# Two residual blocks on one core: evacuating earlier where stages meet, and local attention on three of four key blocks

## The chip, the cores and the metric

The kernel runs on one core of a Trainium2 chip. The metric is the device time of one execution in microseconds, lower is better. A core has TensorE (PE: matmuls; its weight loads are shown apart as PEld), VectorE (DVE), ScalarE (ACT), GpSimd (POOL) and SyncE (SP), each with its own queue of instructions, tied together by semaphores. Here SP issues every large DMA. All data is float32 or float32r.

## The reference

Two blocks for 256 tokens of width 2048. The first has two layers of gated convolution, differential attention with 6 heads and attention on 256 memory tokens with 4 heads. The second, cut to what the change touches:

```python
def second_block(x, c, ...):
    c_act = silu(c)
    mod = c_act @ w_mod + b_mod            # 2048 x 12288: shifts, scales and gates
    h = rms_norm(x, mix_norm_pre) * (1 + sc1) + sh1
    x = x + g1 * rms_norm(token_mixer(h), mix_norm_post)
    h = rms_norm(x, ffn_norm_pre) * (1 + sc2) + sh2
    x = x + g2 * rms_norm(conv_ffn(h), ffn_norm_post)

def token_mixer(h, ...):
    q_a, k_a, v_a, q_b, k_b, v_b, gk, og_b, g_a, g_b = split(h @ w_in)
    # 16 query heads on 4 key heads of width 64; a query sees the 128 keys up to its own position
    o_a = sliding_window_attention(rope(q_a), rope(k_a), v_a, sinks)
    o_b = rms_norm(gated_linear_attention(q_b, k_b, v_b, gk)) * silu(og_b)
    return (sigmoid(g_a) * (o_a @ w_br_a) + sigmoid(g_b) * (o_b @ w_br_b)) @ w_out
```

With 256 tokens the window makes four blocks of 128 queries by 128 keys. The block of the first queries with the last keys is masked out as a whole.

## The kernel before

Activations lie with features on partitions, 128 to a tile, and the 256 tokens along the free axis. The weights, with the modulation matrix most of the 557 MB moved, are read from HBM once and never kept, so the kernel is a stream of **units**: 512 KB of weight, as a rule 512 rows by 256 columns. Each float32 operand is split into a rounded high part and a remainder, and three of the four products are formed: a matmul of 512 columns takes the high weights against both parts of the input, one of 256 columns the low weights against its high part.

A unit passes through four queues. SP loads it into one of 5 buffers `RAW` (L358). ACT copies it, rounded, to `WH` (`act_split`, L540) once the unit four earlier is done. DVE subtracts for `WL` (`dve_split`, L549). PE runs 16 matmuls (L468 and L473; in stages with the tokens on PSUM's partitions 12 matmuls, L415 to L417). There are 4 buffers of `WH` and of `WL`. So when unit w ends, ACT and DVE prepare unit w+4.

Units make **pairs** of output tiles and pairs make **stages**, one for each group of weight columns, in the order mem0, mem1 (keys and values of the memory), then for each layer l qkv, heads_a, heads_b, heads_c, out, then q_a, gk, kv_a, q_b, k_b, v_b0, v_b1, og, g_a, g_b, branch_a, branch_b, mix_out, up0, down0, up1, down1. At a pair's end ACT copies the part made with the input's remainder out of PSUM (`HIGH`, L806) and DVE adds it (`evacuate`, L941 to L964). Both stand behind the split of unit w+4 on their queues.

A stage whose input is another stage's result needs it as `XH`, high part and remainder, in four **input chunks** of four tiles: a copy on ACT (`act_input_chunk`, L1125 or L1131) and a subtraction on DVE (`dve_input_chunk`, L1142 or L1150). There is one `XH`. A chunk is overwritten when the last unit that reads it is done, and `Stage.inside` says how many chunks are made between the last units of the stage before.

Smaller work rides beside the stream at fixed units: attention heads in heads_a to heads_c, 8 turns of local attention in q_b to v_b1 (two query heads a turn), linear attention in og and g_a. The modulation matrix is used up by 192 **modulation steps** on DVE (`dve_modulation`, L1948), each with a load of 512 KB through the same five buffers; `MOD_STEPS` lists the stages and how many steps each has, spread evenly over its units. The order of every queue is that of the Python program, written out by hand.

In a local turn, PE rotates the two query heads and the key head (`pe_rotate`, L1668 to L1671: products with signed permutations), computes the scores of 256 queries by 256 keys (L1239), transposes the probabilities (L1251) and the values (L1255), and multiplies them (L1272). DVE adds the mask (L1327).

## Time and profile before

| | |
|---|---|
| median of 3 runs | 2576.82 us (2576.81 to 2580.57) |
| the profiled execution | 2574.52 us, of which the span is 2572.8 us |
| PE busy, and with weight loads | 2532.5 us (98%), 2169.0 us (84%) |
| DVE, ACT, POOL busy | 1940.7 us (75%), 1297.0 us (50%), 10.8 us |
| DMA | 556.64 MB, mean 216 GB/s |
| granted TensorE clock, mean | 0.998 |

PE counts as busy from a matmul's start to its modelled end, so the few idle stretches are read off the order of time. A row of the timeline gives the start in microseconds from the span's start, a duration, and in brackets how long the engine was idle before it and what ended that.

### The profile page before, as it was taken

Reading aid. Unit: us, or ns where it says so; the run is one execution under the profiler, and the core shown is the slowest. Engines: PE = TensorE matmul, PEld = TensorE weight load, DVE = VectorE, ACT = ScalarE, POOL = GpSimd, SP = SyncE. Lnnn points to the kernel's source line nnn. Section 1 sums busy time; section 2 is a strip of 40 time slices with the busy share of each in tenths; the row PEclk is TensorE's granted clock in tenths of the full one; section 3 lists DMA queues with packets and bytes.
Section 4 is the critical chain, followed back from the end, with each engine's and each line's share of the span. In section 5 each row is a group of like instructions: output and inputs, shape, how many; then the busy total and the mean of one; then the engine's idle time right before and its main releaser. Section 6 shows DMA issues by size and latency. Waiting matters only on the chain.

```text
span 2572.8 us, 35319 instructions
## 1 busy us (share of the span) xinstructions
PE 2532.5 (98%) x13936; PEld 2169.0 (84%) x13936; DVE 1940.7 (75%) x2769; ACT 1297.0 (50%) x1758; POOL 10.8 (0%) x62
## 2 busy tenths in 40 slices
PE   7999999999999999999999999999999999999998
PEld 6888888888888878888788888888888888888886
DVE  6977776887777678676676877886888887788855
ACT  7544556554455555444445554544644443444443
POOL 0000000000000100000000000000000000000000
PEclk9999999999999999999999999999999999999999
DMA  8797454778755466755566888887466668967654
GB/s 277 223 300 246 150 168 152 244 262 282 236 154 166 153 234 221 232 158 152 161 200 209 254 282 275 271 280 266 139 195 191 190 216 301 287 193 204 201 191 140
DMA packets 526519, 556.64 MB, mean 216 GB/s; under 512 B 17409, under 2 KB 453762, under 8 KB 526226
## 3 DMA queue, kind: packets, MB, share of 16 engines
q1 hardware_dynamic: 526354, 554.38, 68.8%
q8 instruction: 110, 1.80, 0.3%
q14 instruction: 55, 0.45, 0.1%
HBM read 552.22 MB, written 2.10 MB: 215 GB/s over the span
## 4 chain that ended last, share of the span: by engine, by line
PE 92%; DVE 5%; ACT 1%; issue 1%; DMA 0%; DVEq 0%; SPq 0%; ACTq 0%
PE ACC L468 45%; PE ACC L473 22%; PE ACC L415 6%; PE ACC L416 6%; PE ACC L417 6%; DVE WL L549 2%; PE SC L1239 1%; PE OU L1272 1%; PE SC L1251 1%; PE SC L1280 1%; DVE XH L1150 1%; DVE XH L1142 0%; ACT WH L540 0%; DVE PR L1574 0%; DVE RAWMOD L1948 0%
## 5 line engine op out<-in xcount | busy, mean ns | idle before, releaser
L468 PE MATMUL ACC<-XH,WH 128*128 128x512 f32 x5296 | 1688.8, 400 | 21.0 <-DVE XH L1150 15.2
L540 ACT ACTIVATE WH<-RAW 128x1024 fp32r<-128x1024 f32 (+1 forms) x852 | 896.9, 1057 | 1089.0 <-PE ACC L473 757.5
L549 DVE TENSOR_TENSOR WL<-RAW,WH 128x1024 fp32r<-128x1024 f32 (+1 forms) x852 | 1032.2, 1220 | 511.9 <-ACT WH L540 510.8
L473 PEld LDWEIGHTS ACC<-XH,WL 128*128 128x128 f32 x5296 | 996.6, 188 | 235.3
L473 PE MATMUL ACC<-XH,WL 128*128 128x256 f32 x5296 | 1043.3, 278 | 0.0
L468 PEld LDWEIGHTS ACC<-XH,WH 128*128 128x128 f32 x5296 | 812.7, 189 | 41.0 <-issue 18.5
L1948 DVE SCALAR_TENSOR_TENSOR RAWMOD<-RAWMOD,CSILU 128x1024 f32<-128x1024 f32 x192 | 234.1, 1219 | 1.5 <-DMA RAWMOD<-in_w_mod_t 1.5
L415 PE MATMUL ACC<-WH,XH 128*128 128x512 f32 x384 | 151.9, 396 | 3.6 <-DVE WL L549 3.6
L416 PE MATMUL ACC<-WL,XH 128*128 128x512 f32 x384 | 149.7, 390 | 0.0
L417 PE MATMUL ACC<-WH,XH 128*128 128x512 f32 x384 | 149.6, 390 | 0.0
L415 PE MATMUL ACC<-WH,AH 128*128 128x512 f32 x352 | 137.4, 390 | 0.0
L417 PE MATMUL ACC<-WH,AH 128*128 128x512 f32 x352 | 137.1, 389 | 0.0
L416 PE MATMUL ACC<-WL,AH 128*128 128x512 f32 x352 | 137.0, 389 | 0.0
L415 PEld LDWEIGHTS ACC<-WH,XH 128*128 128x128 f32 x384 | 72.1, 188 | 22.0 <-issue 7.6
L806 ACT ACTIVATE HIGH<-ACC 128x512 f32<-128x512 f32 (+1 forms) x171 | 89.6, 524 | 0.0
L417 PEld LDWEIGHTS ACC<-WH,XH 128*128 128x128 f32 x384 | 72.1, 188 | 15.3
L416 PEld LDWEIGHTS ACC<-WL,XH 128*128 128x128 f32 x384 | 72.1, 188 | 14.4
L417 PEld LDWEIGHTS ACC<-WH,AH 128*128 128x128 f32 x352 | 66.1, 188 | 13.8
L415 PEld LDWEIGHTS ACC<-WH,AH 128*128 128x128 f32 x352 | 66.1, 188 | 13.5
L416 PEld LDWEIGHTS ACC<-WL,AH 128*128 128x128 f32 x352 | 66.1, 188 | 13.5
L1297 ACT ACTIVATE PROB<-PROB,NM 128x256 f32<-128x256 f32 x80 | 39.7, 498 | 61.3 <-DVE NM L1336 61.3
L941 DVE TENSOR_TENSOR PR<-ACC,HIGH 128x512 f32<-128x512 f32 x64 | 43.8, 685 | 2.1 <-ACT HIGH L806 2.1
(287 smaller groups left out, 1436.3 us busy)
## 6 DMA issues: line engine op xcount, KB each, us to landing
RAW<-in_w_in SPq DMA_DIRECT2D x408, 512.0 KB, 4.5
RAWMOD<-in_w_mod_t SPq DMA_DIRECT2D x192, 512.0 KB, 4.8
RAW<-in_w_up SPq DMA_DIRECT2D x176, 512.0 KB, 4.7
RAW<-in_w_out SPq DMA_DIRECT2D x96, 512.0 KB, 5.5
RAW<-in_w_down SPq DMA_DIRECT2D x88, 512.0 KB, 4.9
RAW<-in_w_mem_kv SPq DMA_DIRECT2D x32, 512.0 KB, 5.9
RAW<-in_w_branch_gla SPq DMA_DIRECT2D x32, 512.0 KB, 5.0
RAW<-in_w_branch_attn SPq DMA_DIRECT2D x16, 512.0 KB, 4.9
```

What stands on the lines that cost most here:

```text
L415: pe.matmul(bank, x, high[:, kc], start=tile == 0, stop=False)
L416: pe.matmul(bank, x, low[:, kc], start=False, stop=False)
L417: mm = pe.matmul(bank, operand[:, tile, T + b * P:T + b * P + P], high[:, kc], start=False, stop=tile == WK * stage.per_pair - 1)
L468: return pe.matmul(bank, k.WH[:, w % RING, kc, cols], x, start=tile == 0, stop=False)
L473: return pe.matmul(bank[:, 0:T], k.WL[:, w % RING, kc, cols], x[:, 0:T], start=False, stop=tile == tiles - 1)
L540: act.activation(k.WH[:, slot, :, 0:width], k.RAW[:, r % RAWS, :, 0:width], ACT.Copy).then_inc(k.hi_ready, 1)
L549: dve.tensor_tensor(k.WL[:, slot, :, 0:width], k.RAW[:, k.plan.unit_load[unit] % RAWS, :, 0:width], k.WH[:, slot, :, 0:width].bitcast(F32) ...
L806: act.activation(k.HIGH[:, first:stage.tiles], k.ACC[:, bank + first:bank + stage.tiles, T:2 * T], ACT.Copy).then_inc(k.high_ready, 1)
L941: chain.link(dve.tensor_tensor(dst, low, high, ALU.add))
L1150: last = dve.scalar_tensor_tensor(out=k.XH[:, f, T:2 * T], in0=prep.source(k)[:, f, :], scalar=prep.gain(k)[:, f:f + 1], in1=hi, op0=ALU.m ...
L1297: last = act.activation(k.PROB[:, g, :], source, ACT.Exp, bias=k.NM[:, g:g + 1], scale=scale, accum_out=k.SM[:, g:g + 1])
L1948: dve.scalar_tensor_tensor(out=raw, in0=raw, scalar=1.0, in1=k.CSILU[:, half * MOD_COLS:(half + 1) * MOD_COLS], op0=ALU.mult, op1=ALU.mult ...
```

## The change

1. **Early evacuation.** `evacuated_early` picks pairs whose `HIGH` and `evacuate` now come ahead of the split of unit w+4: the last pair of mem0, mem1, out0, g_b, branch_a, branch_b and kv_a, and both pairs of the last turn of heads_c. In that turn one DVE split (`held_split`) moves behind the last gate product, and a convolution product (L1580) moves one unit later.
2. **Moved work.** ACT's squares of `x` and DVE's sums of them come three units earlier in mem0. The activation of `c` with its two table loads (`act_small`) goes from mem0 to mem1, and `dve_small` from behind mem0 to behind mem1. Modulation steps keep clear of the first or last units of ten stages.
3. **Input order.** branch_b and mix_out take their input rows in the order 2, 3, 0, 1. branch_a reads only half of `XH`, so the chunks for rows 2 and 3 are made within branch_a at its units 8 and 10.
4. **Local attention.** Scores, mask, exponentials, transposes and values leave out the empty block. Keys are rotated every second turn, values transposed every fourth, from where they lie, without the copy `VS` (dropped in differential attention too).

```diff
 MOD_STEPS = [
-    ("mem1", 6), ("qkv0", 22), ("out0", 16), ("qkv1", 22), ("out1", 12), ("q_a", 8),
+    ("mem1", 3, 8, 12), ("qkv0", 25, 6, 40), ("out0", 16, 4, 27), ("qkv1", 22, 5, 40),
 ...
+LATE_FIRST = (2, 3, 0, 1)
+    by_name["branch_a"].then_first = 2
+    by_name["branch_b"].spots = by_name["mix_out"].spots = LATE_FIRST
 ...
+def held_split(stage, i, w):
+    return stage.beside == "mem" and i == MEM_T // 2 and w == 7
 ...
+def evacuated_early(stage, i, b, q):
+    if q < stage.per_pair - 1:
+        return False
+    final = i == stage.turns - 1 and b == stage.body - 1
+    mixing = stage.beside == "mem" and i == MEM_T // 2
+    return mixing or final and (stage.then is not None or stage.name == "kv_a")
 ...
                 dve_softmax(dve, k, stage, i, w, chain)
-                split_ahead(dve, k, stage, i, w, last, dve_split)
+                early = evacuated_early(stage, i, b, q)
+                if early:
+                    evacuate(i, b)
+                if not held_split(stage, i, w):
+                    split_ahead(dve, k, stage, i, w, last, dve_split)
 ...
-                if stage.name == "mem0" and (i, w) == (1, 2):
+                if stage.name == "mem1" and (i, w) == (0, 6):
                     act_small(act, k)
-                if stage.name == "mem0" and i == 1 and w in (3, 4):
+                if stage.name == "mem0" and i == 1 and w in (0, 1):
                     act.wait_ge(k.x_landed, 64)
-                    for c in (2 * w - 6, 2 * w - 5):
+                    for c in (2 * w, 2 * w + 1):
                         act_squares(act, k, 1, c)
 ...
+                if stage.name == "branch_a" and i == 2 and w in (0, 2):
+                    dve_input_chunk(dve, k, k.preps["ob"], w // 2)
 ...
 def pe_scores(pe, k, kind, u, m=None):
     pe.wait_ge(k.qk_ready, u + 1)
+    if kind == "win":
+        for c in range(2):
+            rows = slice(64 * c, 64 * c + 64)
+            for b in range(2):
+                mm = pe.matmul(k.SC[:, c, window_block(b)], k.QN[rows, 0, P * b:P * b + P],
+                               k.KN[rows, 0, 0:P * (b + 1)], start=True, stop=True)
+        mm.then_inc(k.scores_ready, 1)
+        return
 ...
+def turned_blocks(kind):
+    if kind == "win":
+        return [(c, first, first) for c in range(2) for first in (0, P, 2 * P)]
 ...
+    if kind == "win":
+        for c in range(2):
+            out = k.OU[64 * c:64 * c + 64, 0, 0:T]
+            for kc in range(2):
+                v = k.VT[:, kc * P + 64 * m.parity:kc * P + 64 * m.parity + 64]
+                mm = pe.matmul(out[:, kc * P:], v, k.TURNED[:, c, kc * T:3 * P if kc else T],
+                               start=kc == 0, stop=kc == 1)
 ...
+def values_turned(kind, n):
+    if kind == "diff":
+        return D_V + n
+    return V_A + n // 4 if kind == "win" and n % 4 == 0 else None
 ...
-    pe.matmul(k.SC[:, 0, 0:T], k.ROT[:, :], k.PR[:, O_A + j, :], start=True, stop=True)
-    keys = k.PR[:, K_A + j // 4, :]
-    pe.matmul(k.SC[:, 0, T:2 * T], k.DUP[:, parity, :], keys, start=True, stop=True)
-    pe.matmul(k.SC[:, 1, 0:T], k.DUPROT[:, parity, :], keys, start=True,
-              stop=True).then_inc(k.rotated, 1)
+    mm = pe.matmul(k.SC[:, 0, 0:T], k.ROT[:, :], k.PR[:, O_A + j, :], start=True, stop=True)
+    if j % 2 == 0:
+        keys = k.PR[:, K_A + j // 4, :]
+        pe.matmul(k.SC[:, 0, T:2 * T], k.DUP[:, parity, :], keys, start=True, stop=True)
+        mm = pe.matmul(k.SC[:, 1, 0:T], k.DUPROT[:, parity, :], keys, start=True, stop=True)
+    mm.then_inc(k.rotated, 1)
```

On PE, the second turn of local attention stands thus before; `ROT`, `DUP` and `DUPROT` are the permutations, and the dots are the stream's own matmuls:

```order
L1668 MATMUL SC<-PR,ROT 128x256
L1670 MATMUL SC<-PR,DUP 128x256
L1671 MATMUL SC<-PR,DUPROT 128x256
...
L1239 MATMUL SC<-KN,QN 128x256 x4
...
L1251 MATMUL SC<-IDENT,PROB 128x128 x8
L1255 MATMUL OU<-IDENT,VS 128x128 x2
...
L1272 MATMUL OU<-TURNED,VT 64x256 x4
```

and thus now:

```order
L1769 MATMUL SC<-PR,ROT 128x256
...
L1301 MATMUL SC<-KN,QN 128x128
L1301 MATMUL SC<-KN,QN 128x256
L1301 MATMUL SC<-KN,QN 128x128
L1301 MATMUL SC<-KN,QN 128x256
...
L1328 MATMUL SC<-IDENT,PROB 128x128 x6
...
L1350 MATMUL OU<-TURNED,VT 64x256
L1350 MATMUL OU<-TURNED,VT 64x128
L1350 MATMUL OU<-TURNED,VT 64x256
L1350 MATMUL OU<-TURNED,VT 64x128
```

Both key rotations and both value transposes are gone from this turn, two of the eight transposes of probabilities as well, and two of the four score and value matmuls are half as wide.

On DVE, the last units of heads_c and the first of out stand thus before (`PR<-ACC,HIGH` and `PR<-PR,RSTD` evacuate a pair, `WL<-RAW,WH` is a split, `XH<-PR,XH` an input chunk, `PR<-PR` the gate products L1584 and L1593):

```order
L1142 TENSOR_TENSOR XH<-PR,XH 128x4x256
L549 TENSOR_TENSOR WL<-RAW,WH 128x1024
L1584 TENSOR_TENSOR PR<-PR 128x1024
L1142 TENSOR_TENSOR XH<-PR,XH 128x4x256
L549 TENSOR_TENSOR WL<-RAW,WH 128x1024
L1142 TENSOR_TENSOR XH<-PR,XH 128x4x256
L549 TENSOR_TENSOR WL<-RAW,WH 128x1024
L941 TENSOR_TENSOR PR<-ACC,HIGH 128x512
L943 TENSOR_TENSOR PR<-PR,RSTD 128x512
L1593 TENSOR_TENSOR PR<-PR 128x512
L1142 TENSOR_TENSOR XH<-PR,XH 128x2x256 x2
L549 TENSOR_TENSOR WL<-RAW,WH 128x1024 x2
```

and thus now:

```order
L1189 TENSOR_TENSOR XH<-PR,XH 128x4x256
L564 TENSOR_TENSOR WL<-RAW,WH 128x1024
L1684 TENSOR_TENSOR PR<-PR 128x1024
L1189 TENSOR_TENSOR XH<-PR,XH 128x4x256
L564 TENSOR_TENSOR WL<-RAW,WH 128x1024
L1189 TENSOR_TENSOR XH<-PR,XH 128x4x256
L979 TENSOR_TENSOR PR<-ACC,HIGH 128x512
L981 TENSOR_TENSOR PR<-PR,RSTD 128x512
L1693 TENSOR_TENSOR PR<-PR 128x512
L564 TENSOR_TENSOR WL<-RAW,WH 128x1024
L1189 TENSOR_TENSOR XH<-PR,XH 128x2x256 x2
L564 TENSOR_TENSOR WL<-RAW,WH 128x1024 x4
```

One split, that of the next stage's fourth unit, has moved behind the evacuation and the gate product, so that both come one split earlier.

On DVE at the border of out0 and qkv1, before (`X<-X,SUM` ends the evacuation, `RAWMOD` is a modulation step):

```order
L549 TENSOR_TENSOR WL<-RAW,WH 128x1024
L1948 SCALAR_TENSOR_TENSOR RAWMOD,DERIVED<-RAWMOD,CSILU 128x1024
L1150 SCALAR_TENSOR_TENSOR XH<-X,PARAM,XH 128x256 x4
L549 TENSOR_TENSOR WL<-RAW,WH 128x1024
L1150 SCALAR_TENSOR_TENSOR XH<-X,PARAM,XH 128x256 x4
L549 TENSOR_TENSOR WL<-RAW,WH 128x1024
L1948 SCALAR_TENSOR_TENSOR RAWMOD,DERIVED<-RAWMOD,CSILU 128x1024
L953 TENSOR_TENSOR SUM<-ACC,HIGH 128x512
L964 TENSOR_TENSOR X<-X,SUM 128x512
L1150 SCALAR_TENSOR_TENSOR XH<-X,PARAM,XH 128x256 x4
```

and now:

```order
L564 TENSOR_TENSOR WL<-RAW,WH 128x1024
L1197 SCALAR_TENSOR_TENSOR XH<-X,PARAM,XH 128x256 x4
L564 TENSOR_TENSOR WL<-RAW,WH 128x1024
L1197 SCALAR_TENSOR_TENSOR XH<-X,PARAM,XH 128x256 x4
L991 TENSOR_TENSOR SUM<-ACC,HIGH 128x512
L1002 TENSOR_TENSOR X<-X,SUM 128x512
L564 TENSOR_TENSOR WL<-RAW,WH 128x1024
L1197 SCALAR_TENSOR_TENSOR XH<-X,PARAM,XH 128x256 x4
```

The modulation steps have left the border, and the evacuation stands ahead of the last split.

## Rows read from the trace of the kernel before

**Rows 1.** The page: busy time, chain by engine, groups of splits and modulation.

```profile
PE 2532.5 (98%) x13936; PEld 2169.0 (84%) x13936; DVE 1940.7 (75%) x2769; ACT 1297.0 (50%) x1758; POOL 10.8 (0%) x62
PE 92%; DVE 5%; ACT 1%; issue 1%; DMA 0%; DVEq 0%; SPq 0%; ACTq 0%
L1948 DVE SCALAR_TENSOR_TENSOR RAWMOD<-RAWMOD,CSILU 128x1024 f32<-128x1024 f32 x192 | 234.1, 1219 | 1.5 <-DMA RAWMOD<-in_w_mod_t 1.5
```

**Rows 2.** Timeline, PE: first matmul after each idle stretch between stages.

```profile
60.56 0.70 PE L468 MATMUL ACC<-XH,WH 128*128 128x512 f32 x2 [1.64 <-issue]
65.36 0.73 PE L468 MATMUL ACC<-XH,WH 128*128 128x512 f32 x2 [1.77 <-DVE XH L1150]
472.07 0.73 PE L468 MATMUL ACC<-XH,WH 128*128 128x512 f32 x2 [1.81 <-DVE XH L1142]
565.25 0.73 PE L468 MATMUL ACC<-XH,WH 128*128 128x512 f32 x2 [2.43 <-DVE XH L1150]
923.34 0.47 PE L415 MATMUL ACC<-WH,XH 128*128 128x512 f32 x1 [2.79 <-DVE WL L549]
1090.30 0.70 PE L1668 MATMUL SC<-PR,ROT 128*128 128x256 f32 x2 [0.38 <-DVE PR L946]
1638.80 0.70 PE L468 MATMUL ACC<-XH,WH 128*128 128x512 f32 x2 [1.69 <-issue]
1642.17 0.73 PE L468 MATMUL ACC<-XH,WH 128*128 128x512 f32 x2 [0.35 <-DVE XH L1142]
1740.54 0.47 PE L415 MATMUL ACC<-WH,XH 128*128 128x512 f32 x1 [0.82 <-DVE WL L549]
```

**Rows 3.** Timeline, PE: the pieces of one local turn, and what follows.

```profile
1117.60 0.60 PE L1668 MATMUL SC<-PR,ROT 128*128 128x256 f32 x2
1118.04 0.59 PE L1670 MATMUL SC<-PR,DUP 128*128 128x256 f32 x2
1127.35 1.14 PE L1239 MATMUL SC<-KN,QN 64*128 64x256 f32 x8
1128.42 0.50 PE L468 MATMUL ACC<-XH,WH 128*128 128x512 f32 x1
1136.88 1.04 PE L1251 MATMUL SC<-IDENT,PROB 128*128 128x128 f32 x8
1137.76 0.38 PE L1255 MATMUL OU<-IDENT,VS 128*128 128x128 f32 x2
1140.87 1.09 PE L1272 MATMUL OU<-TURNED,VT 128*64 128x256 f32 x8
```

**Rows 4.** Timeline, weight loads of the same score matmuls.

```profile
1127.34 0.74 PEld L1239 LDWEIGHTS SC<-KN,QN 64*128 64x128 f32 x8
```

**Rows 5.** Timeline, DVE and ACT at the borders.

```profile
63.64 1.66 DVE L1150 SCALAR_TENSOR_TENSOR XH<-Y,PARAM,XH 128x256 fp32r<-128x256 f32 x4
466.70 0.69 DVE L941 TENSOR_TENSOR PR<-ACC,HIGH 128x512 f32<-128x512 f32 x1
470.72 1.29 DVE L1142 TENSOR_TENSOR XH<-PR,XH 128x512 fp32r<-128x512 f32 x2 [1.22 <-ACT XH L1125]
560.34 0.69 DVE L953 TENSOR_TENSOR SUM<-ACC,HIGH 128x512 f32<-128x512 f32 x1
914.45 1.22 DVE L549 TENSOR_TENSOR WL<-RAW,WH 128x1024 fp32r<-128x1024 f32 x1
920.88 3.90 ACT L540 ACTIVATE WH<-RAW 128x1024 fp32r<-128x1024 f32 x4
```

**Rows 6.** Stretches: length, busy PE, PEld, DVE, ACT, POOL (count), clock, DMA share, GB/s.

```profile
10.00:20.00 10.00, 8.95 (x44) 7.77 (x44) 9.21 (x18) 9.29 (x17) 0.00 (x0) 1.00 1.10 353
111.92:225.97 114.05, 114.05 (x654) 98.84 (x653) 93.28 (x121) 51.79 (x58) 0.00 (x0) 1.00 0.87 284
152.00:172.00 20.00, 20.00 (x117) 17.47 (x116) 14.99 (x20) 9.30 (x10) 0.00 (x0) 1.00 0.94 310
1086.98:1303.49 216.51, 216.13 (x1155) 177.24 (x1153) 148.99 (x247) 104.35 (x174) 0.00 (x0) 1.00 0.53 160
```

More of the change, by code:

```diff
@@ L258, in place_modulation @@
     units = []
-    for name, steps in MOD_STEPS:
+    for name, steps, *stretch in MOD_STEPS:
         stage = by_name[name]
-        if isinstance(steps, tuple):
+        if not stretch:
             units += [stage.unit0 + i * stage.units + w for i in range(stage.turns) for w in steps]
             continue
-        length = stage.pairs * stage.per_pair // (2 if name == "mix_out" else 1)
-        units += [stage.unit0 + (2 * j + 1) * length // (2 * steps) for j in range(steps)]
+        first, length = stretch[0], stretch[1] - stretch[0]
+        units += [stage.unit0 + first + (2 * j + 1) * length // (2 * steps) for j in range(steps)]
     assert len(units) == MOD_BLOCKS * KT
@@ L459, in operands @@
             s, tile, tiles = q // 2, 2 * UK * (q % 2) + 2 * kc + h, 4 * UK
+            x = operand[:, tile]
         else:
             s, tile, tiles = h, UK * q + kc, UK * stage.per_pair
-        return (k.ACC[:, bank0 + s], operand[:, tile], s, tile, tiles, kc,
-                slice(h * P, h * P + P))
+            x = operand[:, UK * (stage.spots[q] if stage.inputs is not None else q) + kc]
+        return (k.ACC[:, bank0 + s], x, s, tile, tiles, kc, slice(h * P, h * P + P))
     def high(place, w):
@@ L792, in turn @@
                     act_decays(act, k, w)
-                if stage.name == "branch_a" and w == 2:
-                    act_gate_chunk(act, k, "g_b", G_B, ACT.Sigmoid, k.gb_ready, i)
+                if stage.name == "branch_a" and i < 2 and w in (1, 3):
+                    act_gate_chunk(act, k, "g_b", G_B, ACT.Sigmoid, k.gb_ready, 2 * i + w // 2)
                 if stage.name == "qkv1" and i > 0 and w == 2:
@@ L1033, in turn @@
                     dve_modulation(dve, k, n)
+                if stage.name == "branch_a" and i == 2 and w in (0, 2):
+                    dve_input_chunk(dve, k, k.preps["ob"], w // 2)
                 if last and b == stage.body - 1 and q < stage.inside and stage.then:
-                    dve_input_chunk(dve, k, k.preps[stage.then], q)
-            evacuate(i, b)
+                    dve_input_chunk(dve, k, k.preps[stage.then], stage.then_first + q)
+            if not early:
+                evacuate(i, b)
     stage_turns(stage, turn)
     if stage.then is not None:
-        for c in range(stage.inside, k.preps[stage.then].chunks):
+        for c in range(stage.then_first + stage.inside, k.preps[stage.then].chunks):
             dve_input_chunk(dve, k, k.preps[stage.then], c)
@@ L1166, with __init__ @@
 class Prep:
-    def __init__(self, first, free, chunks, norm, scaled, source, gain, shift, chunk, ready):
+    def __init__(self, first, free, chunks, norm, scaled, source, gain, shift, chunk, ready, free_at,
+                 order):
         self.first, self.free, self.chunks = first, free, chunks
+        self.free_at, self.order = free_at, order
         self.norm, self.scaled, self.source = norm, scaled, source
@@ L1310, in act_copy_turned @@
     else:
-        last = act.activation(k.TURNED[:, :, :], k.SC[:, :, :], ACT.Copy)
-    if kind != "mem":
+        width = 3 * P if kind == "win" else 2 * T
+        last = act.activation(k.TURNED[:, :, 0:width], k.SC[:, :, 0:width], ACT.Copy)
+    if values is not None:
         last = act.activation(k.VT[:, :], k.OU[:, 1, 0:T], ACT.Copy)
```

165 lines of the change are left out of this document (101 added, 64 removed).

## The prediction, made before the changed kernel ran

> **What bounds the kernel.** I read the page's busy shares and its chain first [rows 1]: PE is busy for 98% of the span, and 92% of the chain that ended last runs over PE. A cut elsewhere is worth nothing unless PE waits for it. Two things can pay: instructions taken off PE, and the stretches in which PE stands still. For the second I read PE's timeline for rows with a bracket. Between the first matmul and the last there are few, all where one stage's result is the next one's input. Those that the change touches are in [rows 2], and their brackets sum to 1.64 + 1.77 + 1.81 + 2.43 + 2.79 + 0.38 + 1.69 + 0.35 + 0.82 = 13.68 us. The idle time at the start, at the end, before q_a and before up0 is not touched, and I leave it.
>
> **Local attention on PE.** Over the local turns PE is busy 216.13 of 216.51 us [rows 6], so what goes from PE there goes from the time. In [rows 3]:
> - Key rotations: one product of 256 columns takes 1118.04 - 1117.60 = 0.44 us. Two go in each of four turns: 8 x 0.44 = 3.5 us.
> - Transposes: eight take 1137.76 - 1136.88 = 0.88, so 0.11 each. Two of probabilities go in each of 8 turns, two of values in each of 6, 28 in all: 3.1 us.
> - Scores: four matmuls take 1128.42 - 1127.35 = 1.07 us, or 0.27 each with the start of the group in it. The rows on one half of the partitions run beside those on the other, which without that start would be half of 0.44, 0.22. Two of the four become half as wide: one matmul's worth, 0.22 a turn, 1.8 us in all.
> - Values: the group of the same size (1.09 against 1.14), by the same count 1.8 us.
>
> Sum 10.2 us. The narrow matmuls are the uncertain part. If a matmul of 128 columns costs as much as one of 256, scores and values give nothing and 6.6 us are left; at 0.27 for each they give 4.3 and the sum is 11.0. I take 10.2, since [rows 4] shows the eight weight loads of the scores inside 0.74 us, less than the 1.07 of their matmuls, so that a load doesn't set the pace.
>
> The Trainium skill speaks against this ("TensorE: Matmul & The Clock Gate", section "LDWEIGHTS (loading the stationary operand)"): a load's time goes with its columns and not its rows, about 107 ns for 128. Eight in a row would take 0.86 us however narrow the moving side is, and scores and values would gain nothing. The 0.74 us in [rows 4], with the last load's own duration in it, disagree with that here. It is a rival below.
>
> On DVE a local turn loses the copy of the values, and mask, maximum and scaling become smaller, while one reduction becomes two. DVE is busy for 149 of 216.5 us there [rows 6], so either sign costs nothing. PE's waits in a turn need the scores' inputs three units after the turn begins and the probabilities three units later. With less in front on DVE and ACT both come earlier. In differential attention nothing changes on PE.
>
> **The borders.** qkv0 has 40 units and takes 114.05 us [rows 6], of which the keys and values of the memory are some 2.6, so a unit takes PE 2.79 us. A split takes 1.0 on ACT and 1.22 on DVE, an input chunk of four tiles 1.7 on DVE and as much on ACT, a modulation step 1.22 on DVE [rows 1, 5]. Where PE would have come is the start in [rows 2] less its bracket.
> - mem0 to mem1 (1.64 + 1.77): the first input chunk waited for ACT, which had the table loads, the activation of c and the squares in the last five units, and the second for DVE, which did the sums in front of it and ended it at 63.64 + 1.66 = 65.30 [rows 5]. Now ACT has in each of the last units only a split and a chunk, 1.0 + 1.7 = 2.7 of 2.79 us, and DVE, with a backlog of some 3 us from the sums and an evacuation, ends chunks 0 to 3 about 0.5, 0.5, 2.4 and 1.0 us ahead of PE. All 3.4 go. ACT now waits for x three units earlier, but the loads of x stand in front of that of unit 10, and ACT has split unit 11 by then. Two table loads and three activations move to mem1's unit 6. The four buffers of splits hide them: a split begins three units, 8.4 us, before PE wants it and takes 2.2 on both engines, so some 6 us may come in between.
> - heads_0c to out0 (1.81): the evacuation at 466.70 releases silu, gate product and the last chunk, which ends at 472.01 [rows 5]. One split less in front of it is 1.14, the pair before gives another 0.8 by its own early evacuation, and the chunk then stands behind the held split, whose 1.14 lie beside ACT's two copies. It ends near 470.1, PE comes at 470.3. I count 1.6.
> - out0 to qkv1 (2.43): three modulation steps (3.7 us) and a split leave the front of the evacuation at 560.34 [rows 5]. The last chunk, which ended at 565.2, ends near 560.9, and PE comes at 562.8. All of it goes.
> - heads_1c to out1 (2.79): here the split for out1's fifth unit was late. ACT had waited for silu, table and chunk and began four splits only at 920.88 [rows 5]. With the evacuation some 2 us earlier that split ends near 921.0, PE comes at 920.55. The held split, in [rows 5] done at 915.7, ends near 917.4, PE comes a unit before, at 917.8. 2.3 of 2.79 go; this is the tightest place.
> - kv_a to q_b (0.38): the evacuation is one split earlier. All goes.
> - branch_a to branch_b (1.69 + 0.35): the first two chunks are made eight and six units ahead, the other two have two more units each. All goes.
> - branch_b to mix_out (0.82): a modulation step and a split leave the front of the last evacuation, 2.4 us; the last chunk and ACT's splits behind it come as much earlier. All goes.
>
> Sum 3.4 + 1.6 + 2.4 + 2.3 + 0.4 + 2.0 + 0.8 = 12.9 us. Bounds: 13.7, all the brackets, and, if in each of the seven places 1 us stays, 6.
>
> **What is added.** The modulation steps stay 192, only their places change. The densest is qkv0: 25 steps in 34 units, 59 loads of 524 KB in 94.9 us, 326 GB/s. In [rows 6] the trace has 310 GB/s with a DMA share of 0.94 in that stage, and 353 at the start, where loads queue. At 310 the loads fall 4.9 us behind over the stretch, inside the 6 us that the buffers hold; so nothing, with a bound of 2 us. DVE has there 1.22 + 1.22 x 25/34 + 0.35 (evacuation) = 2.47 of 2.79 us. An early evacuation delays the split behind it by 1.4 us, with those same 6 us above it.
>
> **Sum.** 10.2 + 12.9 = 23.1 us off the profiled execution's 2574.52: 2551.4. The median of the runs stood 2.3 us above that execution, so the median after is near 2554.
>
> **Rivals.**
> - *The stalls move.* At mem0's end DVE has a split and a chunk in each unit, 1.22 + 1.66 = 2.88 us against PE's 2.79, and the held split has 0.3 us to spare. For it speaks that I walk queues with margins of 0.2 to 1 us, in seven places. Against it: the large terms (out0, branch_a, mem0) have over 0.5 us. With about 1 us left in each place the borders give 6, so 16 in all: 2561. With nothing gained at borders: 2566.5.
> - *Narrow matmuls save nothing.* A weight load sets the pace of scores and values: 3.6 us less, 2557.5. This is the skill's rule above; [rows 4] speaks against it.
> - *Slower: DMA can't feed the denser stretches.* In qkv0, out0, qkv1 and branch_b, 198 loads (104 MB) now fall in 119 units, 332 us, 313 GB/s on the mean. Each stretch may fall 6 us behind before PE waits. The gain of 23 is gone when the rate is below 104 / (332 + 4 x 6 + 23) = 274 GB/s, and at 265 the time is 2590. [rows 6] shows 310 in a stretch with loads no sooner wanted, so this is unlikely.
> - *The change doesn't do what it says.* The order of instructions shows the products gone and the evacuations moved; this could only be a hidden wait for a buffer, and is in the first rival.
>
> **Chances.** The forecast, 2551 to 2557: 0.76. Stalls move, 2557 to 2567: 0.15. Narrow matmuls: 0.06. Slower: 0.03. The range 2550.5 to 2563 reaches into the first rival; its low end is the upper bound of the gain (11.0 + 13.7: 2552.1) and 1.6 more, since the 2.3 us between a profiled execution and a median need not be the same (the runs before lie 3.8 apart). About 0.2%, 5 us, is what can be told from no change: faster by more 0.95, within 0.02, slower 0.03.
>
> **What would show it.** The stretch from q_b to v_b1 near 206 us instead of 216.5 with PE busy throughout, of which four turns lose 1.8 us each, two 0.9 and two 0.7; out of the nine brackets at most one or two left, under 1 us each, the likeliest at out1's fourth or fifth unit; qkv0 as long as before, at 2.79 us a unit, though ACT waits more for DMA in it. I am wrong if a new bracket over 1 us stands before a first unit of a stage, if the local stretch is above 209 us, or if qkv0 is over 2 us longer.

## The result, and the profile after

The changed kernel takes 2549.76 us (median of 4 runs, 2549.31 to 2551.72), before 2577.9 in the same comparison: ratio 0.9891, 95% interval 0.9874 to 0.9908, so 1.1% faster. The forecast was 2554.0 with a range from 2550.5; the time lies 0.74 us below that end. The sign was right, the gain was larger than forecast: 23.1 us forecast, 25.1 between the two profiled executions (2574.52 and 2549.41), 28.1 between the medians. Both gaps need a reason.

The page after, busy time, chain and modulation group, the lines that answer to [rows 1]:

```profile
PE 2521.2 (99%) x13892; PEld 2162.1 (85%) x13892; DVE 1927.7 (76%) x2745; ACT 1291.4 (51%) x1752; POOL 10.4 (0%) x63
PE 98%; DVE 1%; DMA 0%; ACT 0%; issue 0%; DVEq 0%; SPq 0%
L2053 DVE SCALAR_TENSOR_TENSOR RAWMOD<-RAWMOD,CSILU 128x1024 f32<-128x1024 f32 x192 | 233.9, 1218 | 0.5 <-DMA RAWMOD<-in_w_mod_t 0.4
```

The chain runs over PE for 98% where it was 92%. In place of the nine brackets of [rows 2] the list of all of PE's waits has only those at the start, before q_a and before up0. Columns: who waited for whom, us in total, times, longest.

```profile
PE ACC L483 <- DVE XH L1197: 11.1, 1, 11.1
PE SC L747 <- DVE PR L952: 4.2, 2, 2.9
PE SC L747 <- DVE WL L564: 0.7, 1, 0.7
PE ACC L456 <- DVE XH L963: 0.2, 1, 0.2
```

The stretches that answer to [rows 6] (same columns): local attention, 10.6 us shorter and PE busy throughout, and qkv0, as long as it was though DMA moves 290 GB/s in it for 284.

```profile
1076.00:1281.90 205.90, 205.90 (x1111) 169.66 (x1109) 139.42 (x235) 98.39 (x168) 0.00 (x0) 1.00 0.56 169
108.69:222.75 114.06, 114.06 (x654) 98.85 (x653) 95.58 (x130) 52.34 (x60) 0.00 (x0) 1.00 0.87 290
```

Measured from the first weight matmul of a stage to that of the next, the stages differ by (us, after less before; those left out by 0.02 or less):

```
mem0 -0.85   mem1 -2.45   out0 -1.82   qkv1 -2.71   out1 -2.84
q_a  +1.18   kv_a -1.57
q_b  -3.02   k_b  -2.64   v_b0 -2.37   v_b1 -2.59
branch_a -1.58   branch_b -0.70   mix_out -1.05   up0 -0.26
```

Borders and local attention account for nearly all. Three of these hold something else, the granted clock. In the kernel before, PE is at half clock (0.50 in the column PEclk, 1.2 GHz for 2.4) for 3.41 us around q_a's beginning and for 3.41 in kv_a; after, for 6.82 us around q_a's beginning and not in kv_a:

```profile
985.00:990.00 5.00, 5.00 (x23) 3.84 (x21) 3.59 (x6) 2.38 (x4) 0.00 (x0) 1.00 0.98 314
992.26:999.08 6.82, 6.10 (x23) 5.31 (x24) 6.51 (x16) 4.90 (x8) 0.00 (x0) 0.50 0.47 156
```

And at the start the first matmuls run at half pace: a pair of 512 columns takes 0.86 us start to start, later 0.46. Before, the pace doubles behind 13.77, after, behind 15.99. That is 0.94 us in mem0's first unit (4.19 and 5.13). The column PEclk reads 1.00 there in both profiles; the half pace is read from the matmuls' starts. PE's timeline, before, then after:

```profile
12.49 1.05 PE L468 MATMUL ACC<-XH,WH 128*128 128x512 f32 x2
13.77 0.69 PE L468 MATMUL ACC<-XH,WH 128*128 128x512 f32 x2
```

```profile
15.13 1.05 PE L483 MATMUL ACC<-XH,WH 128*128 128x512 f32 x2
16.26 0.63 PE L483 MATMUL ACC<-XH,WH 128*128 128x512 f32 x2
```

So the borders gave 0.85 + 0.94 + 2.45 (mem) + 1.82 + 2.71 + 2.84 + 0.38 (in front of q_b) + 1.58 + 0.70 + 1.05 = 15.3 us, for brackets of 13.68, and local attention 10.62 - 0.38 = 10.2.

### The profile page after: what moved, and what is told of

The parts are those of the page before. It is cut to its first block, busy times and chain, and to the rows that moved or that the text cites. A ratio compares the mean times of both kernels' runs of the same rounds, so it can differ in the third digit from the quotient of the medians.

```text
span 2547.6 us, 35203 instructions
## 1 busy us (share of the span) xinstructions
PE 2521.2 (99%) x13892; PEld 2162.1 (85%) x13892; DVE 1927.7 (76%) x2745; ACT 1291.4 (51%) x1752; POOL 10.4 (0%) x63
## 4 chain that ended last, share of the span: by engine, by line
PE 98%; DVE 1%; DMA 0%; ACT 0%; issue 0%; DVEq 0%; SPq 0%
PE ACC L483 49%; PE ACC L488 24%; PE ACC L429 7%; PE ACC L431 7%; PE ACC L430 7%; PE SC L1310 1%; PE OU L1361 1%; PE SC L1328 1%; PE SC L1369 1%; PE ACC L456 0%; PE OU L1833 0%; PE SC L1301 0%; PE OU L1350 0%; PE OU L1498 0%; DVE X L931 0%; DMA RAW<-in_w_mem_kv 0%
## 5 line engine op out<-in xcount | busy, mean ns | idle before, releaser
L483 PE MATMUL ACC<-XH,WH 128*128 128x512 f32 x5296 | 1688.8, 400 | 11.2 <-DVE XH L1197 11.1
L1388 ACT ACTIVATE PROB<-PROB,NM 128x256 f32<-128x256 f32 (+1 forms) x80 | 38.0, 477 | 55.9 <-DVE NM L1435 55.9
```

The costliest lines, as they stand in the source:

```text
L483: return pe.matmul(bank, k.WH[:, w % RING, kc, cols], x, start=tile == 0, stop=False)
L1388: last = act.activation(probs, source, ACT.Exp, bias=k.NM[:, g:g + 1], scale=scale, accum_out=k.SM[:, g:g + 1])
```

## The experiments

All were timed in five rounds beside the kernel before. Each execution lists its mean granted clock, and times go with it: 10 of 59 executions of before show 0.998 and take 2574.5 to 2575.2 us, 13 show 0.997 and take 2576.6 to 2578.1, 34 show 0.996 and take 2577.9 to 2580.7, and 2 show 0.994 and take 2582.8 and 2583.2. Where a few us matter I compare executions of one clock.

### The two halves alone

Local attention of the changed kernel in the kernel before; the changed kernel with the local attention of before; both kernels again. The edits are parts of the diff above, or none.

> The kernel before with the local attention of the changed kernel and none of the moves at stage borders. Mine: the stretch from q_b to v_b1 falls from 216.51 to about 206.3 us (the 0.38 us stop in front of q_b stays), all other stages and all eight other stops stay; 10.2 us less than before. Rival A (the parts help each other, for example a shorter local turn only pays because the borders are free): less than 8 us. Rival B (the 2 us by which the change gave more than forecast lie in local attention, outside the profiled PE rows): more than 12 us between the medians.

> The changed kernel with the local attention of before: only the moves at borders and the modulation steps. Mine: the nine stops go, whose brackets are 13.68 us; each stop also costs some 0.2 us beside its bracket (the profile draws a matmul 0.39 us long though the next one starts 0.23 us after it, and the first matmul after a stop takes 0.31 for 0.23), so 15.5 us less at equal clock. Rival A (forecast as made: brackets alone, and 0.7 of them stay): 12.9 us. Rival B (gains are those of the stage table without any clock correction): 14.5 us. Local attention stays at 216.1 us.

Local attention alone: 2568.62 us, ratio 0.9968 (0.9956 to 0.9981). Borders alone: 2563.61, ratio 0.9948 (0.9935 to 0.9962). The stretches from q_b to v_b1, local part alone, then borders alone:

```profile
1092.84:1299.37 206.53, 206.17 (x1110) 169.68 (x1109) 139.44 (x235) 98.37 (x168) 0.00 (x0) 1.00 0.56 168
```

```profile
1078.36:1294.23 215.87, 215.87 (x1155) 177.09 (x1153) 148.94 (x247) 104.34 (x174) 0.00 (x0) 1.00 0.53 161
```

216.51 - 206.53 = 10.0 us, and the 0.36 of PE's idle time in front of q_b is left. With borders alone, out0, qkv1, branch_a, branch_b and mix_out are as long as in the changed kernel within 0.01 us. They lost 7.86 us for brackets of 1.81 + 2.43 + 1.69 + 0.35 + 0.82 = 7.10.

out1 is the exception, and there both expectations missed. With borders alone one of the nine stops is left, in out1's fifth unit, and the stage is 0.85 us longer than in the changed kernel. With local attention alone the stop there is 2.13 us, not 2.79.

```profile
913.61 0.47 PE L429 MATMUL ACC<-WH,XH 128*128 128x512 f32 x1 [0.60 <-DVE WL L564]
```

So the local half gives some 0.65 us at this border. The way leads over GpSimd and DVE. At the end of heads1c GpSimd builds the window mask, which the change makes smaller (384 columns for 512), and DVE does six convolution steps beside it. They take 3.55 us in before and with borders alone, 2.9 with local attention alone and in the changed kernel. DVE's timeline, before, then after:

```profile
892.81 3.55 DVE L1574 SCALAR_TENSOR_TENSOR PR<-CU,PARAM,PR 128x256 f32<-128x256 f32 x6
885.05 2.89 DVE L1674 SCALAR_TENSOR_TENSOR PR<-CU,PARAM,PR 128x256 f32<-128x256 f32 x6
```

In the first layer, where GpSimd does nothing at that time, six such steps take 2.46 us in before. That GpSimd's work is what slows them fits all of this; no run changes the mask alone.

By stages (mem0 corrected for its start, as above) borders alone give 14.7 us and local attention alone 10.0 + 0.7 = 10.7, together 25.4 for the 15.3 + 10.2 of the changed kernel. So the halves add up, and neither needs the other but for this 0.65 us. The medians give 14.3 and 9.3 us. That they are 0.4 and 1.4 us short is within what half-clock stretches do: the profile of local attention alone has 20 us of them, that of borders alone 10, the two of before 7 and 17.

> The kernel before, unchanged, for a second profile. It differs from its first profile only in where TensorE is granted half its clock. Mine: stage lengths are the same within 0.1 us wherever the granted clock is 1.0, and the stretches at 0.5 have moved, come or gone; they explain the distance between the profiled execution (2574.52 us) and the median of the runs (2577.9): about 3 us, two half-clock stretches of 3.4 us more than the first profile had. Rival: the distance lies in the frame around the span (before the first and after the last instruction), with the clock's stretches the same.

> The changed kernel, unchanged, for a second profile. Mine: all nine stops are gone again; q_a's extra 1.2 us and kv_a's missing 1.6 us, which follow the stretches at half clock, come out another way; everything else stays within 0.1 us. Rival: q_a is longer and kv_a shorter by the change itself, and the same numbers return.

Before, again: 2579.18 us, ratio 1.0006 (0.9997 to 1.0015), profiled execution 2579.31 with a span of 2577.6. After, again: 2551.99 (4 runs, 2549.34 to 2555.23), ratio 0.9901 (0.9887 to 0.9914), span 2547.7. The second profile of after repeats the first, q_a's half-clock stretch and all: my theory that it would come out another way fell, and the rival's numbers returned. What speaks against the rival are other profiles: borders alone and `dense` (below) have the same edits around q_a and kv_a, and there q_a takes 48.66 and 48.64 us for 48.91 and kv_a 27.69 for 26.14, with 3.41 us at half clock in each. Two of after's four runs are 5 us longer, at clock 0.996. The second profile of before has five half-clock stretches where the first has two, and differs in nothing else but the start (mem0 0.69 us longer): mem1, qkv1 and out1 are longer by 1.25, 1.56 and 1.53 us. One begins 1.2 us behind the end of the stop of 2.42 us in qkv1:

```profile
565.40:568.10 2.70, 1.10 (x6) 0.97 (x7) 2.48 (x5) 2.70 (x4) 0.00 (x0) 1.00 0.21 79
568.16:571.57 3.41, 3.41 (x13) 2.92 (x12) 3.41 (x5) 0.87 (x1) 0.00 (x0) 0.50 0.55 163
571.58:575.00 3.42, 3.42 (x18) 2.99 (x18) 2.76 (x5) 2.44 (x4) 0.00 (x0) 1.00 0.98 318
```

One begins at the end of out1's stop (926.56; PE goes on at 926.65), and one in mem1 0.6 us behind the end of its second stop (65.84):

```profile
66.40:69.81 3.41, 3.41 (x12) 2.93 (x11) 3.34 (x8) 1.90 (x4) 0.00 (x0) 0.50 0.50 153
```

The profile of local attention alone has one there too, 1.5 us behind that stop. None of the 12 profiles of kernels with the changed borders, other than those with the early evacuation or the squares undone (below), has a half-clock stretch at mem1, out0, qkv1 or out1's fifth unit. The frame around the span is 1.7 to 1.8 us in all profiles. So the 2.3 us that I had put between profile and median are half-clock stretches, and the stops that the change removes had been bringing some of them.

### Parts undone

> The changed kernel, but in local attention all scores and value products are 256 columns wide again (the values of the second key block are read from the wrong place, so the output is not the reference's; the number and size of the instructions is what counts). Key rotations, transposes, mask and borders stay as changed. Mine: 0.22 us for scores and 0.22 for values in each of eight turns, the stretch from q_b to v_b1 goes from 205.89 to 209.4, 3.5 us more. Rival (a weight load sets the pace, so narrow products save nothing): the stretch stays at 205.9.

```diff
-                mm = pe.matmul(k.SC[:, c, window_block(b)], k.QN[rows, 0, P * b:P * b + P],
-                               k.KN[rows, 0, 0:P * (b + 1)], start=True, stop=True)
+                mm = pe.matmul(k.SC[:, c, P * b:P * b + T], k.QN[rows, 0, P * b:P * b + P],
+                               k.KN[rows, 0, 0:T], start=True, stop=True)
 ...
-                mm = pe.matmul(out[:, kc * P:], v, k.TURNED[:, c, kc * T:3 * P if kc else T],
+                mm = pe.matmul(out, v, k.TURNED[:, c, kc * P:kc * P + T],
```

2557.49 us, ratio 0.9919 (0.9905 to 0.9932). The stretch of local attention:

```profile
1079.18:1288.46 209.28, 209.28 (x1111) 171.00 (x1109) 139.37 (x235) 98.60 (x168) 0.00 (x0) 1.00 0.55 166
```

3.38 us more than 205.90 in eight turns, 0.42 each; I had forecast 0.44. The rest of the difference of the medians is half-clock stretches. A narrow product is worth what its columns say. In the changed kernel the eight weight loads of a turn's scores stand inside 0.53 us (those of [rows 4] took 0.74), so they got faster with the products. Timeline, PE and PEld, the row that answers to L1239 of [rows 3], and its loads:

```profile
1114.22 0.93 PE L1301 MATMUL SC<-KN,QN 64*128 64x128 f32 x8
1114.22 0.53 PEld L1301 LDWEIGHTS SC<-KN,QN 64*128 64x128 f32 x8
```

The Trainium skill ("TensorE: Matmul & The Clock Gate", section "LDWEIGHTS (loading the stationary operand)") has a load's time go with its 128 columns whatever its rows. The loads of this group begin in pairs, one for each half of the partitions, 0.01 us apart, and the four pairs follow each other by 0.11 us: 0.53 less the last load's own 0.19 is 0.34, three such steps. So here that time holds for a pair of loads and not for each, and a pair of products of 128 columns, 0.11 us too, just keeps its pace. My rival had counted eight loads one behind the other.

> The changed kernel with every evacuation back behind the split of the unit, and no held split. Mine: stops come back where the prediction gave the early evacuation as the cause: out0 1.6 to 1.8 us, out1 2.0 to 2.8, q_b 0.38, together 4.5 to 5.5 with 0.2 for each; at qkv1 and mix_out, where modulation steps were taken away too, 0 to 1 each; mem0 and branch_a none. Sum about 6 us at equal clock. Rival (modulation steps and chunk order did the work, the early evacuation hides in slack): under 2 us.

```diff
 def evacuated_early(stage, i, b, q):
-    ...
+    return False
 def held_split(stage, i, w):
-    return stage.beside == "mem" and i == MEM_T // 2 and w == 7
+    return False
```

2559.13 us, ratio 0.9929 (0.9916 to 0.9941). The stops that came back, all of them:

```profile
468.66 0.50 PE L483 MATMUL ACC<-XH,WH 128*128 128x512 f32 x1 [1.80 <-DVE XH L1187]
918.13 0.47 PE L429 MATMUL ACC<-WH,XH 128*128 128x512 f32 x1 [2.13 <-DVE WL L564]
1088.44 0.70 PE L1765 MATMUL SC<-PR,ROT 128*128 128x256 f32 x2 [0.38 <-DVE PR L982]
```

out0, out1 and q_b, as expected, 4.3 us of brackets. out0 became 3.38 us longer for its 1.80, since a half-clock stretch began at 469.87. At mem0, qkv1, branch_a and mix_out nothing came back: there the other edits are enough by themselves.

> The changed kernel with the squares of x, their sums and the activation of c back where they were, in the last units of mem0 and in front of mem1. Mine: the two stops at mem0/mem1 come back, shorter than the 1.64 and 1.77 us of before by the evacuation that is still early: 2 to 3.4 us of brackets and 0.25 for each stop; nothing else moves but the stretches at half clock. Rival (the early evacuation alone had removed them): no stop over 0.3 us there and the same time.

```diff
-                if stage.name == "mem1" and (i, w) == (0, 6):
+                if stage.name == "mem0" and (i, w) == (1, 2):
                     act_small(act, k)
-                if stage.name == "mem0" and i == 1 and w in (0, 1):
+                if stage.name == "mem0" and i == 1 and w in (3, 4):
 ...
```

2553.97 us, ratio 0.991 (0.9896 to 0.9923). The stops of before return at full length although the evacuation is early, with a third behind them:

```profile
60.40 0.47 PE L483 MATMUL ACC<-XH,WH 128*128 128x512 f32 x1 [1.63 <-issue]
65.19 0.50 PE L483 MATMUL ACC<-XH,WH 128*128 128x512 f32 x1 [1.76 <-DVE XH L1197]
74.08 0.50 PE L483 MATMUL ACC<-XH,WH 128*128 128x512 f32 x1 [0.98 <-DVE XH L1197]
```

At clock 0.998 that is 2553.9 against 2549.4, 4.5 us. The squares, sums and activation of c, which this run moves back together, did all of this border.

> The changed kernel with the modulation steps of qkv0 to out1 and of g_b to mix_out spread evenly over their stages again, in the same numbers (the last units and those behind a border are no longer free of them). Mine: a step of 1.22 us stands again in front of the last evacuation; stops of 0.3 to 2.4 us come back at qkv1 and 0.3 to 0.8 at mix_out, 1 to 3 us together; out0 and out1 stay as changed, since their borders have no step in front. Rival (the steps' places don't matter once the evacuation is early): no stop, same time.

```diff
-    ("mem1", 3, 8, 12), ("qkv0", 25, 6, 40), ("out0", 16, 4, 27), ("qkv1", 22, 5, 40),
+    ("mem1", 3, 8, 12), ("qkv0", 25, 0, 40), ("out0", 16, 0, 32), ("qkv1", 22, 0, 40),
 ...
```

2553.66 us, ratio 0.9905 (0.9892 to 0.9919); the one run at 0.998 takes 2550.33, 0.9 more than the changed kernel. A stop of 0.55 us came back at qkv1 and none at mix_out: that stage is 0.30 us longer without idle time of PE at its border, and branch_a 0.27 shorter; what moved there is not known. At qkv1 PE comes at 556.9 and the last chunk ends at 555.76 + 1.67 = 557.4 (DVE's timeline), because one modulation step stands between split and chunk:

```profile
553.48 1.22 DVE L564 TENSOR_TENSOR WL<-RAW,WH 128x1024 fp32r<-128x1024 f32 x1
554.61 1.22 DVE L2053 SCALAR_TENSOR_TENSOR RAWMOD<-RAWMOD,CSILU 128x1024 f32<-128x1024 f32 x1
555.76 1.67 DVE L1197 SCALAR_TENSOR_TENSOR XH<-X,PARAM,XH 128x256 fp32r<-128x256 f32 x4
557.35 1.22 DVE L564 TENSOR_TENSOR WL<-RAW,WH 128x1024 fp32r<-128x1024 f32 x1
```

### More load, and stops by themselves

> The changed kernel with 30 instead of 25 modulation steps in qkv0's 34 units, and 17 instead of 22 in qkv1: 64 loads (33.5 MB) in 94.9 us, 353 GB/s wanted. Mine: the queue gives up to 350 GB/s when it is behind, as in the first 10 us of the kernel, so qkv0 stays at 114.06 us or grows by at most 1 us. Rival (the 310 GB/s seen in that stage before is its limit): the loads fall 13 us behind, less 6 to 8 us that the buffers hold, and qkv0 is 5 to 7 us longer. DVE has 2.65 of 2.79 us per unit and is not the limit.

```diff
-    ... ("qkv0", 25, 6, 40), ... ("qkv1", 22, 5, 40),
+    ... ("qkv0", 30, 6, 40), ... ("qkv1", 17, 5, 40),
```

2552.98 us, ratio 0.99 (0.9886 to 0.9913). Neither theory: qkv0 stays at 114.06, but heads0a behind it grows by 2.99, with two stops. The loads came at 316 GB/s for the 353 wanted (first row, over the 34 units), ACT waited 55.3 us for DMA in them (38.4 in the changed kernel), and the stops came just behind the stage's end:

```profile
124.60:219.00 94.40, 94.40 (x541) 81.67 (x540) 79.04 (x105) 40.59 (x43) 0.00 (x0) 1.00 0.93 316
...
227.11 0.70 PE L1369 MATMUL SC<-SQ,HALVES 128*128 128x512 f32 x1 [2.24 <-DVE SQ L1718]
234.24 0.49 PE L1310 MATMUL SC<-KN,QN 64*128 64x256 f32 x2 [0.41 <-DVE KN L1732]
```

By my estimate 3.6 of the 33.5 MB wanted in 94.9 us were late, 11 us at 316 GB/s, and the buffers hid all but 3. DVE was busy for only 79.04 of 94.40 us in the first row, so over the stage its own work was not the limit. But at the first stop PE waits for DVE, which had worked since 216.85 with hardly a break, and late loads and DVE's own work are not separated there. So denser steps do cost, and the change stops at most five steps short of it. The forecast's DMA rival needed under 274 GB/s; the rate here was above that.

> The changed kernel with nine stops added where it has none: in front of heads0a, b, c, heads1a, b, c, og, g_a and g_b, PE waits until GpSimd has done five small chained memsets, which begin when PE ends the stage before. Mine: each stage with a stop becomes longer by the stop's bracket and 0.2 to 0.3 us, and behind some of the nine stops a stretch at half the granted clock begins within 4 us, which costs 1.5 to 1.7 us more; about a third of them, so 3 such stretches, other ones in each execution. With brackets b the time grows by 9 x (b + 0.25) + 3 x 1.6. Rival A: a stop costs its bracket alone, 9 x b. Rival B: half-clock stretches come at fixed places (before q_a, in kv_a, up0) and not at added stops: 9 x (b + 0.25).

```diff
+def pe_stop(pe, k, name):
+    if name in STOPS:
+        pe.wait_ge(k.held, STOPS.index(name) + 1)
+def pool_stops(pool, k, names, chain):
+    for name in names:
+        pool.wait_ge(k.unit_done, k.plan.s[name].unit0)
+        for n in range(5):
+            chain.link(pool.memset(k.HOLD[:, :], 1.0))
+        pool.sem_inc(k.held, 1)
```

> The kernel with nine added stops, each made longer: 14 chained memsets on GpSimd instead of 5, so brackets of about 2.4 us (two of the nine 2.0 and 1.7) instead of 0.2 to 1.0. Mine now: it is the length of a stop that decides. Behind two to five of the nine a stretch at half clock begins within 4 us, each 1.5 us more, so the time is that of the changed kernel plus the brackets, nine times 0.17, and 3 to 7 us. Rival (the place decides: only stops that fall together with an input change or low-row work bring one): no half-clock stretch near the nine, as with the short stops, and the time is brackets plus 1.5 us.

```diff
-        for n in range(5):
+        for n in range(14):
```

Short stops: 2558.95 us, ratio 0.9926 (0.9914 to 0.9939). Long: 2580.14, ratio 1.0011 (1.0002 to 1.002). PE's waits in the one, then in the other:

```profile
PE ACC L483 <- POOLq L2221: 6.3, 9, 1.0
```

```profile
PE ACC L483 <- POOLq L2221: 20.5, 9, 2.6
```

The stages around the short stops grew by 7.75 us for brackets of 6.33: 0.16 us a stop beside its bracket. None of the nine is followed by a half-clock stretch; the three in that profile are at q_a, in kv_a and at up0, as in most. Of the nine long stops, two are. They begin 0.19 us behind the stop of 1.76 us in front of og, and within that of 2.56 in front of g_a:

```profile
1404.00:1405.30 1.30, 0.00 (x0) 0.00 (x0) 1.24 (x3) 1.28 (x3) 0.88 (x8) 1.00 0.77 201
1405.31:1408.72 3.41, 2.90 (x9) 2.52 (x10) 1.03 (x2) 3.23 (x4) 0.29 (x3) 0.50 0.66 222
1408.73:1412.00 3.27, 3.27 (x20) 2.83 (x19) 0.62 (x1) 3.23 (x4) 0.00 (x0) 1.00 0.01 4
```

Stages grew by 24.88 us for 20.5 of brackets, so 4.4 beside them: 9 x 0.16 and 2.9 for the two stretches. So added stops do bring such stretches, against the rival. Length seems to matter: stops up to 1.0 us brought none of nine, those of 1.76 to 2.56 two of nine. One profile of each is thin for a rate, but the other executions point the same way: all eleven with long stops show a mean clock of 0.994 or less, all five with short ones 0.996 or 0.997. The stop of 1.76 brought one while the six of 2.13 and 2.56 ahead of it did not, so length is not all that decides.

The Trainium skill (same page, section "HAM oscillation — how this bites in real kernels") describes a matmul stream that loses its full clock because PE waits for loads between its pieces. These rows agree in kind, for a stream that is over 98% busy.

### Filling the idle time

> The changed kernel with matmuls of constants that nobody reads while PE would stand still: 44 (128 columns each) before mem0 and 24 behind out1, in front of q_a. Mine: the granted clock follows what PE does, so mem0 starts at full clock (1.4 to 2.5 us less) and the stretch at half clock at q_a goes (3.1 us less); 4.5 to 5.5 us less than the changed kernel, and the runs lie closer together. Rival (the half-clock stretches come at fixed times, or from the wait and not from idleness): mem0 no shorter, q_a's stretch stays; 0.

```diff
+    pe_keep_warm(pe, k, s["mem0"], 44)
     pe_stage(pe, k, s["mem0"])
 ...
+    pe_keep_warm(pe, k, s["q_a"], 24)
     for f in range(4):
         pe_turn_normed(pe, k, 0, f)
```

2553.91 us, ratio 0.9903 (0.9888 to 0.9918), 4 us longer than the changed kernel, because I had reckoned 0.11 us for a product and it takes twice that, and four times that at the half pace of the start: the 44 lasted 12.8 us, where 8 were free, and mem0 began at 15.8 instead of 11.1. The clock did what was expected: mem0 took 46.40 us for 48.66 and q_a 47.18 for 48.91, without a half-clock stretch.

> The kernel with the extra matmuls and two more edits: the 16 records (3.5 us in one piece) of the products with only 16 rows in kv_a are spread between the products of its second unit, and before up0 there are 42 instead of 32 idle-time matmuls. Mine: half-clock stretches in kv_a and at up0, which most executions show, go or get rare: the median falls 1.5 to 4 us below that of the kernel with the extra matmuls alone, and the lowest time stays. Rival (rows don't matter, the stretch in kv_a comes by chance of timing): kv_a stays at 29.3 us in as many profiles and the medians are the same.

```diff
-                if stage.name == "kv_a" and w == 1:
-                    pe_decays(pe, k)
 ...
                     mm = low(both[1], w)
+                    if stage.name == "kv_a" and w == 1:
+                        pe_decays(pe, k, n)
```

2553.14 us, ratio 0.9904 (0.989 to 0.9917), no half-clock stretch behind the start in its profile and three of four runs at clock 0.999. But kv_a took 27.30 us for 26.14 (after's profile has none there either): small products between the others cost 1.16 us in place of the 1.6 or 3.1 of the stretch.

> The changed kernel with idle-time matmuls in the right number: 21 before mem0, 12 in front of q_a, 37 instead of 32 in front of up0 (a product of fp32 with 128 columns is two records, 0.21 us at full clock and 0.43 at half). Mine: mem0 is 46.4 us long and begins at 11.1 as in the changed kernel; q_a is 47.2 long with out1 at 93.7; the lowest time is 2549.3 - 2.3 - 1.7 - 0.7 = 2544.6 us, the median 2545 to 2548, since kv_a's half-clock stretch of 1.6 or 3.1 us still comes in some executions. Rival (the matmuls delay what they should cover, as in the first try): 2549 or more.

```diff
-WARM = 32
+WARM = 37
 ...
+    pe_keep_warm(pe, k, s["mem0"], 21)
 ...
+    pe_keep_warm(pe, k, s["q_a"], 12)
```

> The same, with the products of 16 rows in kv_a in two pieces of 1.8 us, behind the stage's first unit and its second, in place of one of 3.5 us. Mine: kv_a has no half-clock stretch and is 26.2 us long (spread over one unit they had cost 1.16 us in switching); the median equals the lowest time within 1 us, near 2545. Rival (a piece of 1.8 us is enough to bring it): kv_a at 27.7 or 29.3 in the profile, and the runs spread over 3 us as with the other.

```diff
-                if stage.name == "kv_a" and w == 1:
-                    pe_decays(pe, k)
+                if stage.name == "kv_a" and w < 2:
+                    pe_decays(pe, k, w)
```

With the right counts: 2547.77 us (2546.18 to 2549.65), ratio 0.9881 (0.9865 to 0.9897), and with the 16-row products in two pieces 2547.18 (2546.95 to 2548.31), ratio 0.9878 (0.9864 to 0.9892). Of their 8 runs 7 are below the changed kernel's lowest time of 2549.31, and the medians are 2.0 and 2.6 us below its 2549.76, so this small step is real. It is less than forecast (2544.6): PE now reaches mem0's first units before their input. It waits 1.69 us behind the extra matmuls, the first four units take 3.24, 3.02, 3.02 and 2.89 us in place of 2.79, and mem0 is 47.33 long instead of 46.40. PE's timeline at the start, and the stretch at q_a, now at full clock:

```profile
3.25 6.45 PE L761 MATMUL ACC<-ONES,IDENT 128*128 128x128 f32 x42 [3.25 <-POOL ONES L2107]
11.38 0.74 PE L483 MATMUL ACC<-XH,WH 128*128 128x512 f32 x2 [1.69 <-DVE XH L1201]
...
990.00:1000.00 10.00, 8.84 (x62) 7.67 (x61) 9.25 (x22) 8.15 (x16) 0.00 (x0) 1.00 0.33 109
```

The pieces did not do what they were for. The profile with two pieces has a half-clock stretch of 3.41 us at 1052.81 in kv_a (28.20 us long), that with one piece has none. Whether halving helps stays open.

## Why the prediction was wrong

The time lies 4.2 us under the forecast: 2.0 us because more went than was counted, 1.9 because the median moved towards the profiled execution (0.35 above it, not 2.3), and 0.3 from rounding up 2553.7.

- **Local attention, 10.2 us: right**, 10.2 measured without the stop in front of q_b, 10.0 with local attention alone. Scores and values, which I called the uncertain part, gave 3.4 for 3.6; rotations and transposes the other 6.8 for 6.6, by subtraction. The turns lose 2.64, 2.37 and 2.59 us in pairs.
- **The borders, 12.9 us: the term that was mis-sized.** It measured 15.3. Part of it are stops that I had let stand, 0.8 us. At out0 I counted 1.6 of 1.81: the chunk ended at 465.67 + 1.29 = 466.96, the 470.1 of the forecast less the 3.23 us by which the stage began earlier, and PE came at 467.02 (DVE, first row). At out1 I let 0.5 stand, since the evacuation would come some 2 us earlier. For the border edits that was right: with borders alone ACT's four splits begin 2.2 us earlier than in before, and a stop of 0.60 is left. In the changed kernel they begin at 910.31, in before's time 918.1 instead of 920.88 [rows 5], 2.8 us earlier, and the split is ready 0.15 us ahead of PE (ACT, second row). The rest is the local half's, by DVE's shorter convolution steps, a path that was in no step of mine: I had put the smaller mask at nothing.

```profile
465.67 1.29 DVE L1189 TENSOR_TENSOR XH<-PR,XH 128x512 fp32r<-128x512 f32 x2
...
910.31 3.91 ACT L555 ACTIVATE WH<-RAW 128x1024 fp32r<-128x1024 f32 x4
```

- The other part of it, 1.6 us, was in no step: **a stop costs more than its bracket.** The bracket begins where the profile lets the last matmul end, 0.39 us behind its start, but the next one would have started 0.23 behind it. I read brackets as time lost. The nine stops that went give 0.18 each, the nine added short ones 0.16.
- **"The median of the runs stood 2.3 us above that execution": failed.** I carried this distance over as if it belonged to the measurement. It is half-clock stretches, of which the stops brought some: after stands 0.35 above its profile, before 3.4. At equal clock (0.998) the gain is 2574.76 - 2549.41 = 25.3 us (medians of 10 and 5 executions). From all executions (59 and 8) it is 2578.2 - 2549.8 = 28.4. The 3 us between are half-clock stretches that before has more of. Three stand at removed stops in its second profile; for the other executions, which have no profile, that this is where they come from is not shown.
- The early evacuation was needed where I had rested the sum on it (out0, out1, q_b). For mem0 I named squares, sums and the activation of c, and together they did it without the early evacuation. For qkv1 I named steps and a split, and undoing either left at most 0.55 of 2.43. The new input order (item 3 of the change) was not undone by itself, so what it gives at branch_b and mix_out is not separated.
- **What is added, 0: right**, but nearer to its bound than thought: 25 steps cost nothing in qkv0, 30 cost 3 us just behind it.
- Of the rivals none came. The range's low end took in 1.6 us beyond the bounds of the sum; the two causes above needed 2.3.

## What to carry to other kernels

Price a stop of the busiest engine at its bracket plus the modelled tail of the last matmul (here 0.16 to 0.18 us), and where it is long (here 1.76 us and more) add a chance of 1.5 us at half clock. Before carrying over a distance between profile and median, ask whether the change touches what makes it: list time against granted clock for all runs, and compare at equal clock. When a border is tight by several small causes, undo one at a time; here only three of the seven needed the early evacuation, and one was closed in the end by an edit made for another stage.

## What the runs showed of the hardware

- Half-clock stretches lasted 3.41 or 6.83 us wherever the 17 profiles show one (that at the program's end apart; two profiles show no other), and cost 1.2 to 1.6 us for each 3.41 in which PE had work. They came at or behind stops of 1.76 us or more (mem1, out0, qkv1, out1, og, g_a, in front of q_a) and at up0's two of 1.29 and 0.75 us. They also came in kv_a, where PE is never idle, 2.3 to 4.8 us behind the beginning of its products with 16 of 128 rows: in 11 of the 15 profiles that have these in one piece of some 3.5 us. That few rows make it is not shown: spread out they brought none in one profile, in two pieces one in one.
- The first matmuls at half pace ended 2.8 us behind PE's start in one profile and 4.9 in another, 0.9 us of difference by chance alone; over the 13 profiles without extra matmuls there it is 2.8 to 6.1. Matmuls that nobody reads, in PE's free time ahead, took it away.
- A product of 128 fp32 columns is two records, 0.22 us at full clock and 0.43 at half.
- Six convolution steps on DVE took 2.46 us with GpSimd idle and 2.89 or 3.55 beside its memsets and selects, the longer where these are wider.
